# The tail of a two-block transformer: token tile 0 of the last layer runs up to its first expert selection, and tile 1's products follow

## The reference

```python
def second_block(x, ...):
    xn = rms_norm_2(x, ln_mix_g[l])
    proj = xn @ w_in[l]
    a_out = gmlp_spatial_gating(proj[..., :a0], proj[..., a0:a1], ...)   # u, v
    b_out = banded_chunk_attention(proj[..., q0:k0], proj[..., k0:v0], proj[..., v0:], ...)
    x = x + jnp.concatenate([a_out, b_out], axis=-1) @ w_out[l]
    x = x + peer_ffn(rms_norm_2(x, ln_ffn_g[l]), peer_w_query[l], peer_sub_keys[l], peer_u[l], peer_v[l])

def peer_ffn's block(xb):                       # 128 tokens
    q = (xb @ w_query).reshape(128, 8, 2, 128)   # 8 heads
    sc = jnp.einsum('thpd,hpkd->thpk', q, sub_keys)
    s_top, i_top = lax.top_k(sc, 16)
    ... best, pos = lax.top_k(cand, 16); eidx = ...; g = softmax(best)
    h = gelu(einsum('thk,..', peer_u[eidx], xb)); out = sum g * h * peer_v[eidx]
```

## Time and profile before

| | us |
|---|---|
| median of three runs (lowest to highest) | 1212.51 (1212.46 to 1213.06) |
| profiled execution: its time, its span | 1212.02, 1210.2 |
| busy in the span: PE, DVE, ACT, POOL | 1057.7, 804.7, 614.1, 336.8 |
| DMA queue q0 (gathers mostly), share of the 16 engines over the span | 54.8% |
| first gather issued on POOL, at | 550.46 |

### The profile page before, as it was taken

One profiled execution on the slowest core, in us unless ns is written; L12 is line 12 of the kernel. 1 busy time (PEld: TensorE's weight loads), 2 busy tenths in 40 slices (PEclk: granted clock), 3 DMA queues, 4 the chain that ended last, 5 costly groups with the idle time before them and its releaser, 6 DMA issues.

```text
span 1210.2 us, 12529 instructions
## 1 busy us (share of the span) xinstructions
PE 1057.7 (87%) x3744; PEld 657.2 (54%) x3744; DVE 804.7 (66%) x1677; ACT 614.1 (51%) x1339; POOL 336.8 (28%) x284
## 2 busy tenths in 40 slices
PE   6999999999999999999887988677778777887686
PEld 5788878888878787876333443223323322333232
DVE  5763766755555687567877667766776677667744
...
DMA  8463447865535654348999999999999999999995
GB/s 314 141 208 106 138 141 239 272 209 182 182 99 189 232 193 141 139 132 333 422 420 422 421 421 421 422 421 421 422 419 415 413 422 421 402 413 421 422 421 243
DMA packets 95253, 369.53 MB, mean 305 GB/s; under 512 B 6545, under 2 KB 30105, under 8 KB 62305
## 3 DMA queue, kind: packets, MB, share of 16 engines
q0 software_dynamic: 38176, 273.46, 54.8%
...
...
HBM read 367.81 MB, written 1.06 MB: 305 GB/s over the span
## 4 chain that ended last, share of the span: by engine, by line
PE 49%; DMA 26%; DVE 14%; ACT 5%; issue 4%; POOL 2%; DVEq 0%; SPq 0%; ACTq 0%; POOLq 0%
DMA uv_ring<-in_peer_uv,expert 26%; PE gemm L1360 11%; PE gemm L1691 11%; PE gemm L1362 11%; PE gemm L1361 11%; DVE uv_ring L1276 4%; POOL uv_ring L415 2%; PE trb L1354 1%; DVE w_lo L784 1%; ACT diag L754 1%; PE mmb L1440 1%; PE mmb L1481 1%; ACT w_hi L437 1%; DVE hit L1266 1%; DVE hit L1264 1%
## 5 line engine op out<-in xcount | busy, mean ns | idle before, releaser
L1691 PE MATMUL gemm<-uv_ring,diag 128*128 128x512 f32 x1024 | 497.5, 630 | 127.2 <-ACT diag L754 126.8
L1691 PEld LDWEIGHTS gemm<-uv_ring,diag 128*128 128x128 f32 x1024 | 191.3, 198 | 421.3 <-ACT diag L754 244.4
L1276 DVE CUSTOM_DVE_ANT_0 uv_ring<-uv_ring,xn 128x1024 f32<-128x1024 f32 x256 | 309.9, 1222 | 160.1 <-DMA uv_ring<-in_peer_uv,expert 157.3
L415 POOL DMA_INDIRECT uv_ring<-in_peer_uv,expert x256 | 320.1, 1250 | 321.3 <-PE gemm L1691 296.4
L784 DVE TENSOR_TENSOR w_lo<-raw,w_hi 128x1024 fp32r<-128x1024 f32 (+1 forms) x201 | 213.5, 1075 | 153.1 <-ACT w_hi L437 152.7
L437 ACT ACTIVATE w_hi<-raw 128x1024 fp32r<-128x1024 f32 (+1 forms) x204 | 189.1, 940 | 189.3 <-PE gemm L1362 187.2
L1360 PE MATMUL gemm<-w_hi,hT_hi 128*128 128x512 f32 (+1 forms) x608 | 246.1, 405 | 12.8 <-DVE w_lo L784 12.6
L1362 PE MATMUL gemm<-w_hi,hT_lo 128*128 128x512 f32 (+1 forms) x608 | 236.1, 388 | 0.0
L1361 PE MATMUL gemm<-w_lo,hT_hi 128*128 128x512 f32 (+1 forms) x608 | 235.8, 388 | 0.0
L748 ACT ACTIVATE hid_g<-hid,scales 128x1 f32<-128x1 f32 x256 | 75.1, 293 | 311.4 <-DVE hid L1276 309.3
L1360 PEld LDWEIGHTS gemm<-w_hi,hT_hi 128*128 128x128 f32 x608 | 114.7, 189 | 40.5 <-DVE w_lo L784 14.0
...
...
## 6 DMA issues: line engine op xcount, KB each, us to landing
...
uv_ring<-in_peer_uv,expert POOLq DMA_INDIRECT x256
```

Source lines behind the costliest of these rows:

```text
L415: nc.gpsimd.indirect_dma_start(out=uv_ring[k % RING][:], out_offset=None, in_=peer_uv, in_offset=bass.IndirectOffsetOnAxis(ap=expert[:, n, ...
L1276: V.tensor_tensor_reduce(out=u_row, in0=u_row, in1=xn[:, b, :], scale=1.0, scalar=0.0, op0=ALU.mult, op1=ALU.add, accum_out=hid[par][:, k: ...
L1691: last = nc.tensor.matmul(gemm[2 * b + n][:], diag[k % 4][:], uv_ring[k % RING][:, D + n * CHUNK:D + (n + 1) * CHUNK], start=(begin and k ...
```

## The change

- Chunk 44 is multiplied tile by tile, and the pieces that stood behind it (turned probabilities, gate, values of tile 0, mixed columns) stand between its quarters. The gate's v columns are now chunk 42 and the attention's values chunk 43; the square root and Gelu steps of the gate move up with them.
- The split second output chunk has places of its own (`out2_split`), and so has the split first half of chunk 47 (`first_split`), the 256 columns of head 0. With `w_hi`/`w_lo` three split chunks are held at once, and each can serve tile 0 and, later, tile 1.
- PE makes both output chunks for tile 0, turns its norm columns, makes head 0's queries and scores, and only then the output products, norm columns and queries of tile 1. The second half of chunk 47 (head 1) follows; chunks 48 to 50 of both tiles all stand between the rows of heads 0 to 4 (before: half of chunk 49, and chunk 50).
- Remainders of these chunks move from DVE to POOL: quarters 2 and 3 of the second output chunk, 4 half quarters of chunk 47, and 12 quarters between gathers of heads 0, 1 and 3.
- The loads of chunks 49 and 50 wait for later remainders. Ring places 4 to 7 lie elsewhere, and the first, seventh and eighth gather have new waits.

```diff
-        uv_at = [AT_BIG + 2 * D * i for i in range(5)] + [AT_SPARE, AT_RAW + RAW // 2, AT_RAW + RAW // 2 + 2 * D]
+        uv_at = [AT_BIG + 2 * D * i for i in range(4)] + [AT_ARENA + 8192, AT_SPARE, AT_BIG + 10240, AT_ARENA + 2048]
...
+        out2_split = [[at(f"out2_{name}{q}", place, [P, 1024], f32r) for q, place in enumerate(places)] for name, places in (
+            ("hi", (AT_BIG + 5120, AT_BIG + 6144, AT_BIG + 7168, AT_SPARE)),
+            ("lo", (AT_ARENA + 8192, AT_ARENA + 9216, AT_SPARE + 1024, AT_ARENA)))]
+        first_split = [[at(f"first_{name}{q}", place, [P, 2, HEAD_Q], f32r) for q, place in enumerate(places)] for name, places in (
+            ("hi", [AT_ARENA + 6144 + 512 * q for q in range(4)]),
+            ("lo", (AT_ARENA + 3072, AT_ARENA + 3584, AT_BIG + 11264, AT_BIG + 11776)))]
...
-        IN2_COLS = [D, D + CHUNK, 2 * D, HALF, 0]
+        SQUARES = numbered(("norm1", 4), ("norm2", 4), ("final", 8), ("gate", 2), ("norm4", 4))
+        ALL_SQUARES = SQUARES["norm4"] + 4
+        IN2_COLS = [D, D + CHUNK, HALF, 2 * D, 0]
...
-            for n in range(4):
-                load(C_QUERY + n, (C_QUERY + n) % 2, peer_w_query_2[0], n * CHUNK)
+            load(C_QUERY, 1, peer_w_query_2[0], 0)
+
+            def load_query(n, half):
+                sp.dma_start(raw[:, (C_QUERY + n) % 2, half, :].rearrange("p (k n) -> p k n", k=KD // 2),
+                             peer_w_query_2[0].rearrange("(k p) n -> p k n", p=P)[:, half * 4:half * 4 + 4, n * CHUNK:(n + 1) * CHUNK]
+                             ).then_inc(w_landed[(C_QUERY + n) % 2][half], 16)
+
+            for half in range(2):
+                sp.wait_ge(out2_lo_ready[half], 2)
+                load_query(1, half)
+            for half in range(2):
+                sp.wait_ge(first_lo_ready, 2 * half + 2)
+                sp.wait_ge(lo_ready, 4 * M_SECOND + 2 * half + 2)
+                load_query(2, half)
+            for half in range(2):
+                sp.wait_ge(lo_ready, 4 * (M_SECOND + 1) + 2 * half + 2)
+                load_query(3, half)
...
+            for q in (2, 3):
+                pool.wait_ge(out2_hi_ready, q + 1)
+                nc.gpsimd.tensor_tensor(out2_split[1][q][:], raw[:, 0, 1, (q % 2) * 1024:(q % 2 + 1) * 1024],
+                                        out2_split[0][q][:].bitcast(f32), ALU.subtract).then_inc(out2_lo_ready[1], 1)
+
+            query_remainders(0, range(4))
+
+            between = {(0, 8 + q): (1, q) for q in range(4)}
+            between.update({(1, k): (2, q) for q, k in enumerate((11, 12, 13, 15))})
+            between.update({(3, 1 + q): (3, q) for q in range(4)})
 
             for n in range(TB * PEER_HEADS):
                 pool.wait_ge(expert_ready, n + 1)
                 for k in range(TOPK):
                     pool.wait_ge(row_free, n * TOPK + k + 1)
+                    if n == 0 and k == 0:
+                        pool.wait_ge(g_filled[1], C_OUT2 + 2)
                     if n == 0 and k == 6:
-                        pool.wait_ge(lo_ready, 4 * (C_QUERY + 3))
+                        pool.wait_ge(g_filled[1], FILLED_FIRST)
+                    if n == 0 and k == 7:
+                        pool.wait_ge(squared, ALL_SQUARES)
                     nc.gpsimd.indirect_dma_start(
                         out=uv_ring[k % RING][:], out_offset=None, in_=peer_uv,
                         in_offset=bass.IndirectOffsetOnAxis(ap=expert[:, n, k:k + 1], axis=0),
                     ).then_inc(row_landed[k % RING], 16)
+                    if (n, k) in between:
+                        query_remainders(between[n, k][0], (between[n, k][1],))
 
 
...
+            out2_hi((0,))
+            gmlp_u(0)
+            one_hi_columns("mixed_10", 1, 0)
+            hi_at(C_OUT2, quarters=(0,))
+            probs_columns((2, 3))
+            hi_at(C_OUT2, quarters=(1,))
+            probs_columns((4, 5))
+            hi_at(C_OUT2, quarters=(2,))
+            one_hi_columns("mixed_00", 0, 0)
+            hi_at(C_OUT2, quarters=(3,))
+            gmlp_u(1)
             nc.scalar.preload_act_table(ACT.Sqrt)
-            hi_at(C_OUT2 + 1)
-            for b in range(TB):
-                residual_in(C_OUT2, b)
-                squares(b, 0)
-            norm_behind("norm4", C_OUT2 + 1)
+            out2_hi((1, 2, 3))
+            one_hi_columns("mixed_01", 0, 1)
+            residual_in(C_OUT2, 0)
+            squares(0, 0)
+            first_hi((0,))
+            one_hi_columns("norm4_00", 0, 0)
+            first_hi((1, 2, 3))
+            residual_in(C_OUT2 + 1, 0)
+            squares(0, 1)
+            one_hi_columns("norm4_10", 1, 0)
+            root_of("norm4", 0)
+            one_hi_columns("mixed_11", 1, 1)
...
+            def first_query():
+                scaled("norm4", 1)
+                act.wait_ge(g_filled[0], FILLED_FIRST)
+                nc.scalar.activation(neg_dist[:], gemm[2][:, 0:HEAD_Q], ACT.Copy, scale=query_scale(0)).then_inc(g_free[2], 1)
+                t = TR["first_q"]
+                act.wait_ge(tr_filled, t + 1)
+                for i, turned in enumerate((age, q_pos)):
+                    ins = nc.scalar.activation(turned[:], trb[t % 2][:, i * P:(i + 1) * P], ACT.Copy)
+                ins.then_inc(tr_out[t % 2], 1)
+                m = MM["first_s"]
+                act.wait_ge(mm_filled, m + 1)
+                nc.scalar.activation(tk_work[:], mmb[m % 2][:, 0:2 * P], ACT.Copy).then_inc(mm_out[m % 2], 1)
...
-            weigh(0, 0, 0, after={4: last_hi(0), 6: last_hi(1), 11: last_hi(2), 15: lambda: queries_out(2, 0)})
...
+            weigh(0, 0, 0, after={0: split(1, 0), 1: split(1, 1), 2: split(1, 2), 3: split(1, 3), 4: taken(0, 1), 7: turned(0, 1), 9: scored(0, 1),
+                               12: taken(1, 0), 15: turned(1, 0)})
+            weigh(1, 1, 0, after={1: scored(1, 0), 2: split(2, 0), 3: split(2, 1), 4: split(2, 2), 5: taken(1, 1), 6: split(2, 3), 8: turned(1, 1), 10: scored(1, 1)})
...
+                gained(b, half, peer_row)
+
+            def peer_scale(b):
+                inverse_root(b, 1, RS["norm4"] + b, dst=scales[:, SC_PEER + b:SC_PEER + b + 1], done=scale_ready)
+
+            band_out(0)
+            gate_out(0)
+            gate_out(1)
+            one_lo_columns("mixed_10", 1, 0)
+            gated(0)
             lo_at(C_OUT2, quarters=(0, 1))
-            band_out(0)
-            lo_columns("mixed", (0, 1))
+            one_lo_columns("mixed_00", 0, 0)
             lo_at(C_OUT2, quarters=(2, 3))
+            gated(1)
+            one_lo_columns("mixed_01", 0, 1)
+            out2_lo((0, 1))
+            out2_row(0, 0)
+            one_lo_columns("norm4_00", 0, 0)
+            first_lo((0, 1))
+            out2_row(0, 1)
+            first_lo((2, 3))
+            variance("norm4", 0)
+            one_lo_columns("norm4_10", 1, 0)
+            peer_scale(0)
             band_out(1)
-            lo_columns("mixed", (2, 3))
-            lo_at(C_OUT2 + 1)
-            me.settle()
-            residual(C_OUT2, 0, scale=SC_FINAL)
-
-
-            norm_behind("norm4", C_OUT2 + 1, peer_row, SC_PEER, SC_FINAL)
-            lo_at(C_QUERY + 1, quarters=(0,))
+            one_lo_columns("mixed_11", 1, 1)
...
+            select(0, 0, scored(MM["first_s"]), loaded=True)
+
+            out2_row(1, 0)
+            out2_row(1, 1)
+            one_lo_columns("norm4_01", 0, 1)
+            one_lo_columns("norm4_11", 1, 1)
+            variance("norm4", 1)
+            peer_scale(1)
...
+            product_at(C_IN2 + 4, by_tile=True, before={
+                (0, 0): lambda: score_band((4, 5)), (1, 0): lambda: turn_band_probs((0, 1)), (3, 0): lambda: band_values(0),
+                (0, 1): gate, (1, 1): lambda: (mixed_columns(1, 0), turn_band_probs((2, 3))), (2, 1): lambda: turn_band_probs((4, 5)),
+                (3, 1): lambda: mixed_columns(0, 0)})
...
+            for q in range(4):
+                if q == 2:
+                    mixed_columns(0, 1)
+                out2_a(q, 0)
+            for q in range(4):
+                if q == 2:
+                    norm4_columns(0, 0)
+                out2_b(q, 0)
+            band_values(1, range(0, 4))
+            norm4_columns(1, 0)
+            band_values(1, range(4, HEADS))
+            first_part(0, 0)
+            first_part(1, 0)
+            mixed_columns(1, 1)
+            first_part(2, 0)
+            first_part(3, 0)
+            out2_a(0, 1, (0,))
+            pe.wait_ge(g_free[2], FREED_OUT2[1] + 1)
+            turn(TR["first_q"], [neg_dist[:, i * P:(i + 1) * P] for i in range(2)])
+            out2_a(0, 1, (1,))
+            tr_ready(TR["first_q"])
+            pe.wait_ge(keys_landed, 16)
+            bank = mm_bank(MM["first_s"])
+            for i, turned_q in enumerate((age, q_pos)):
+                last = nc.tensor.matmul(bank[:, i * P:(i + 1) * P], turned_q[:], keys_t[:, i, :], start=True, stop=True)
+            last.then_inc(mm_filled, 1)
+            for q in range(1, 4):
```

(24 more changed lines are left out.)

435 lines of the change are left out of this document (261 added, 174 removed), and 3 rows, old and new, of the table TR.

## The result

| | before | after |
|---|---|---|
| median, us (lowest to highest, 20 runs each) | 1212.47 (1211.42 to 1213.71) | 1215.89 (1211.88 to 1218.48) |
| ratio to before (95% interval) | | 1.0022 (1.0016 to 1.0028) |
| profiled execution: time, span | 1212.02, 1210.2 | 1216.42, 1214.7 |
| first gather issued, us | 550.46 | 537.95 |

What follows compares the result with a forecast made beforehand. The gather stream through the DMA engines was taken to bound the kernel. 1212.0 - 13.3 (earlier first gather) + 5.1 (weights) + 3.0 (ring) = 1206.8, with the median 0.5 above the profiled run: 1207.0 us, range 1200.5 to 1213.

Steps and rivals of the forecast that it cites:

- Term 1: Front, before the first gather: PE's new order starts head 0's `select` at 525.2 instead of 538.5, 13.3 us earlier.
- its 536 to 539: Sign named for the front: the first gather is issued between 536 and 539 us.
- The walk's own side case: Front: POOL's two new remainders hold DVE's two, second output chunk 2.2 us later, `select` at 526.2 instead of 524.0.
- Term 2: Full gather stream: chunk 50's 2.1 MB of weights now cross it, costing 5.1 us, ends 4.5 and 6.5.
- Term 3: Ring of gathers in the settled stage: delays from PE, POOL and DVE might run it dry; 0 to 10 us, 3 taken.
- The step on the cover: Gather ring: 8 us of work queued in the DMA engines lets a round be delayed up to 8 us at no cost.
- DVE loses its four remainders and gains time: Settled gather stage: DVE is rid of four remainders, 4.7 us of work, and so gains time.
- POOL's sum: Between gathers: issue 1.6 plus remainder 2.4 is 4.0 us against 2.49 of stream; four in a row, 6 us behind.
- PE is full but at most 1 us behind: Heads 0 to 2: rows and query pieces take PE 40, 41 and 38 us against DMA's 40 a head, plus weight loads.
- The exclusion rival: Bursts of four remainders in heads 0, 1 and 3: remainder and dot exclude each other, remainders lengthen, 1226 us; chance 12%.
- The mean wait of 0.6 us: Argument against exclusion: a dot fills half the time, so a remainder likelier waits 0.6 us than 2.4; 8.4 a burst.
- the sign that would refute it: Gather stage: dips summing to over 6 us refute the forecast; dots over 1.3 or remainders over 3 us point to exclusion.

Runs made afterwards that it cites:

- the run with four in head 7: Four remainders of chunk 50 made once more on POOL behind gathers 1 to 4 of head 7, against the kernel with twelve remainders on DVE: 1206.97 us.

## Why the prediction was wrong

**Term 1 was right.** 13.3 us were predicted, 12.5 came; `select` began at 526.15, and the first gather stood inside its 536 to 539. The walk's own side case, that POOL's two remainders hold DVE's two, gives 526.2, and the hold did happen: DVE's second took from 507.6 to 511.0, and PE waited 1.8 and 1.7 us for them (total us, times, longest):

```profile
PE gemm L1547 <- DVE out_lo L1367: 3.5, 2, 1.8
```

That the sum meets the trace so closely is in part luck. The side case puts 2.2 us on the hold; with all four remainders on DVE the first gather came 0.6 us sooner, and 1.6 with the row between them.

**Term 2 was right in kind.** 5.1 us were put on it, and SP's queue moved 2.1 MB more. The run with 16 of the 512 columns gave 3.9 by the medians and 4.5 by the ratios, some 2 to 7.

**Term 3 failed, in its cover and in its line on DVE.** 3 us were taken and 12.4 were lost. The step on the cover was "the difference, 8 us, ... a delay of up to 8 us in a round of the ring costs nothing", with a burst that is 6 us behind "under the 8". The 8 came from one gather, the 12th of head 1, whose dot starts 15.0 us after its issue. At a head's start the lead is shorter. In the kernel before, gather 1 of head 3 and gather 1 of head 7, issue and dot:

```profile
669.89 0.96 POOL L415 DMA_INDIRECT uv_ring<-in_peer_uv,expert  x1 [0.32 <-PE gemm L1691]
681.24 1.25 DVE L1276 CUSTOM_DVE_ANT_0 uv_ring<-uv_ring,xn 128x1024 f32<-128x1024 f32 x1 [1.26 <-DMA uv_ring<-in_peer_uv,expert]
...
832.11 0.94 POOL L415 DMA_INDIRECT uv_ring<-in_peer_uv,expert  x1 [2.12 <-PE gemm L1691]
842.38 1.23 DVE L1276 CUSTOM_DVE_ANT_0 uv_ring<-uv_ring,xn 128x1024 f32<-128x1024 f32 x1 [1.25 <-DMA uv_ring<-in_peer_uv,expert]
```

11.4 and 10.3 us, so a cover of 4.9 and 3.8 by the same subtraction. Bursts stood there (head 3) or ran into it (the end of head 1; gather 0 of head 2 has a lead of 7.5 in after). The burst of fills in head 3, where no dot was held, is a test of this: 8.6 behind and 3.4 lost leave a cover of 5.2. In the run with four in head 7 the burst was 6.6 us behind (four gathers from 823.33 to 839.96 against 10.0 of stream). The same kernel without it has a lead of 11.1 there (823.64 to 834.76), a cover of 4.6; that explains 2.0 of the 4.6 us missed. The other 2.6 may be DVE, which had 2.0 + 1.5 + 2.8 = 6.3 us of held dots there; this part is argued, not shown.

**Three more steps of term 3 failed with it, and the first cost most.**
- "DVE loses its four remainders and gains time": it lost 18.7 us by being held. With fills, which hold no dot, 3.4 us are missing instead of 12.4.
- POOL's sum counted issues and remainders, but no wait at the head of its queue. Where each split stands on ACT was in the code, and against the gather it was never laid. Where the four stand, with this wait in it, made 4.7 of the 5.8 us of the second stretch.
- "PE is full but at most 1 us behind" held, but a full PE also means that nothing is caught up: that made 5.0 of the 6.6 us of the first stretch. The shares overlap, as either the held dots or the full PE taken away ends most of it.

**The exclusion rival**, that remainder and dot exclude each other, had the mechanism and the sign, and 12% of the chance. Its price was on the wrong engine: it made the remainders longer (a limit at 3.9 us; measured 2.45) and gave 1226 (7.8 beyond the cover three times is 23.4, not 22, so 1228 by its own numbers). The mean wait of 0.6 us that stood against it was worked out for POOL; DVE's was 1.6 a remainder. The Trainium skill, "SBUF — State Buffer", section "Who interferes with whom", lets the one that issues first keep the shared ports and the other block for the whole instruction. The trace agrees for both dots above: they start 0.4 and 0.2 us behind a remainder and take 3.4 us. It does not for the step of `select` at 621.85, which starts 0.34 us ahead of the remainder at 622.19 by the records and is held all the same. It isn't alone: the dot at 832.43 in the run with four in head 7 starts 0.58 us ahead of the remainder at 833.01 and takes 4.03. The same section of the Trainium skill also says that an instruction that only writes doesn't contend with two inputs of DVE's, which the fills bear out, dots at 1222 ns.

The text named the sign that would refute it, dips of more than 6 us in heads 0, 1 and 3 with dots over 1.3, and these came in heads 1 and 3 (and 2 behind 1). Head 0's burst cost nothing that shows: 416 GB/s from 560 to 600 us, the same as in the kernel with DVE's remainders.

One more sum of the text is off, without weight here: half of its 7.0 us of waits is 18.0 us earlier, not 17.5.
